# Dilated attention of a two-block layer stack: two small groups in one score tile by token class, 64x64 score matmuls, stacked values

## The chip, the cores and the metric

The kernel runs on one core of a Trainium2 chip. The metric is the device time of one execution in microseconds (us). The engines are called as the profile calls them: PE (the matrix engine; PEld is its weight load), DVE, ACT, POOL, and SP, which only issues transfers here.

## The reference, cut to what matters

Two blocks of two layers each run on 256 tokens of width 1024. The change is in the second block, whose layers are "hybrid": one projection feeds a gated convolution, an MLA attention of 8 heads and a dilated attention of 8 heads in three groups.

```python
DIL_PATTERNS = ((128, 1), (512, 4), (2048, 16))   # window, dilation
outs, lses = [], []
for gi, (window, dilation) in enumerate(DIL_PATTERNS):
    o_g, lse_g = dilated_group_attention(dq[:, :, gi], dk[:, :, gi], dv[:, :, gi], slopes[gi],
                                         dilation, window // dilation)
alpha = jax.nn.softmax(jnp.stack(lses, axis=0), axis=0)
o_c = jnp.sum(alpha[..., None] * jnp.stack(outs, axis=0), axis=0)
```

In a group of dilation d a query sees the keys whose distance is a multiple of d (at most 128 steps back), with a bias of minus slope times distance. Weighting the groups by the softmax of their log-sums equals one softmax over the scores of all three groups. With 256 tokens, a query of dilation 4 sees only keys of its own class mod 4 (64 tokens), and a query of dilation 16 only some of the same 64.

## The kernel before, in words

All activations are kept transposed (features on the 128 partitions, 256 tokens along the free side). A projection block is a 128x1024 piece of weights: SP fetches it into `raw`, ACT rounds it to `whi`, DVE makes the rest `wlo`, and PE runs 8 x 3 matmuls of 256 columns into a `G` slot (L513 to L515, in the function `run`). Values are made with tokens on the partitions by `run_tokens` (L572 to L574): two banks of `G`, one for each half of the tokens, from four weight blocks; ACT copies them to `dv` with `evac_tokens` (L1210). For the dilated heads, tokens are split by parity: ACT writes `dq`, `dk` even tokens first (L1573, L1574), and `run_tokens(by_parity=True)` reads every second token of `h` as its stationary operand.

The attention of a hybrid layer is one loop of 17 steps on PE (`for i in range(17)`), with blocks of other projections (`BESIDE[i]`) between: step i has the scores of head i (0 to 7 MLA, 8 to 15 dilated), the transposes of the weights of head i-1, and every second step `pair_outs`, weights times values for two heads. For a dilated head:

- POOL makes the biases (L489), one head ahead.
- `dil_scores` (L1089): group 0 needs every key, so 2 matmuls of 128x256; groups 1 and 2 need keys of the query's parity, so 2 of 128x128 each. The contraction is 64 deep; group 0 lies in one half of PE's rows and groups 1 and 2 in the other.
- DVE's `minima` (L2316) adds the bias, writes 1024 columns of `sn` and takes the minimum; ACT's `exps` (L1621) takes the exponential and its sum; DVE's `normalise` (L2330) scales.
- `to_keys` (L966) transposes 8 squares of 128x128, ACT copies them to `pt2` (L1660), and `pair_outs` (L1120) accumulates in `O`: for each of two heads, which take PE's left and right 64 columns, 2 matmuls of 256 columns for group 0 and 4 of 128 for groups 1 and 2.

A matmul on plain 32-bit operands (scores, values) runs on PE as two passes, and the trace has a row for each pass; transposes have one. After the loop come 36 merge blocks and the output projection. `settle` runs two small matmuls before the long runs. PE, DVE and ACT each work off their own list in the order of the code; semaphores join them.

Of the kernel before, what the change touches and what calls it, by code (L numbers as in the profile page):

```python
# [25 lines left out]
T = 256  # L26
P = 128
# [59 lines left out]
ORDER = (1, 0, 2)  # L87
SLOPES = [2.0 ** (-8.0 * (n + 1) / 24) for n in range(24)]

HYB_S = 4 + 4 + 8 + 24  # L90
# [34 lines left out]
for _f in range(FT):  # L125
# [10 lines left out]
WEIGHT_TILES = ((256, 768, 384, 896), (0, 512, 128, 640))  # L136
DIST = (slice(0, 512), slice(512, 768), slice(768, 1024))
PLACES = [((slice(0, T), slice(0, T)), (slice(T, 2 * T), slice(512, 768))),
          ((slice(0, P), slice(T, 384)), (slice(P, T), slice(768, 896))),
          ((slice(0, P), slice(384, 512)), (slice(P, T), slice(896, 1024)))]  # L140


def spans(i):

    return (slice(0, 512), slice(512, 1024)) if i >= 8 else (slice(0, P), slice(P, 384))


def even_odd(ap):

    return ap.rearrange("p (i two) -> p two i", two=2)  # L150


def score_uses(i):

    return 8 + min(i + 1, 8) + 3 * max(0, i - 7)
# [39 lines left out]
def build(nc, a, out):  # L195
# [8 lines left out]
    with ctx:  # L204
# [85 lines left out]
        dist = sb("dist", [P, 1024], stack=second)  # L290
# [10 lines left out]
        bias = sb("bias", [P, 1024], stack=second)  # L301
        pt2 = sb("pt2", [P, 2, 1024], stack=second)
        mn2 = sb("mn2", [P, 2, 2, 3], stack=second)
# [16 lines left out]
        u = yh[:, 4:12, :]  # L320
        s32 = sb("s32", [P, 32], stack=second)
# [13 lines left out]
        for n, t in (("o_dist", [P, 1024]), ("o_bones", [P, P]), ("o_lcs", [P, 2, 2, 16]),  # L335
                     ("o_rows", [P, LAYERS2, 2, 96])):
            sb(n, t, stack=mh_stack)
# [6 lines left out]
        for n, t in (("o2_dist", [P, 1024]), ("o2_bones", [P, P]), ("o2_lcs", [P, 2, 2, 16]),  # L344
                     ("o2_rows", [P, LAYERS2, 2, 96]), ("o2_dqk", [P, 24, T]), ("o2_dv", [P, 2, 1536])):
            sb(n, t, stack=sq2)
# [44 lines left out]
        bias_ready = sem("bias_ready")  # L391
        weights_ready = sem("weights_ready")
# [74 lines left out]
        def _(pool):  # L467
# [13 lines left out]
            with pool.Fori(0, LAYERS2) as l:  # L481
                for j in range(24):
                    head, grp = j // 3, ORDER[j % 3]

                    k = j - 3
                    pool.wait_ge(s_free, L1_S + l * HYB_S + (score_uses(8 + k // 3) - 2 + k % 3 if j >= 3 else 0))
                    c = 8 * grp + head
                    w = DIST[grp].stop - DIST[grp].start
                    pool.tensor_tensor(bias[:, DIST[grp]], dist[:, DIST[grp]], slopes[:, c:c + 1].broadcast_to([P, w]),  # L489
                                       ALU.mult).then_inc(bias_ready, 1)  # L490


        @block.tensor
        def _(pe):
# [58 lines left out]
            def run_tokens(b, g, j, b4=0, g4=0, by_parity=False):  # L553
# [3 lines left out]
                for jj, tt in {0: ((0, 0), (0, 1)), 1: ((1, 0), (1, 1)), 2: ((2, 0),), 3: ((3, 0), (2, 1), (3, 1))}[j]:  # L557
# [7 lines left out]
                    for kk in range(2):  # L565
                        k = 2 * jj + kk
                        if by_parity:
                            hh, hl = even_odd(h[:, k, 0:T])[:, tt, :], even_odd(h[:, k, T:2 * T])[:, tt, :]
                        else:
                            hh, hl = h[:, k, tt * P:(tt + 1) * P], h[:, k, T + tt * P:T + (tt + 1) * P]  # L570
# [375 lines left out]
            for l in range(LAYERS2):  # L946
# [118 lines left out]
                for j in range(12):  # L1065
                    run_tokens(B_HYB + H_DV + j // 4 * 4, G_HYB + H_DV + j // 4 * 4, j % 4, b4, g4, by_parity=True)
# [11 lines left out]
                def dil_scores(head):  # L1078
# [3 lines left out]
                    places = {0: (3 * p + 2 * e, 64 * e), 1: (3 * p + e, 64 - 64 * e), 2: (3 * p + 1 + e, 64 - 64 * e)}  # L1082
                    slots = {}
                    for grp, qt in ((1, 0), (0, 0), (1, 1), (0, 1), (2, 0), (2, 1)):
                        if qt == 0:
                            slots[grp] = use_s()
                        t, o = places[grp]
                        tile = slice(qt * P, (qt + 1) * P)
                        ins = pe.matmul(S[:, slots[grp], PLACES[grp][qt][0]], dqk[o:o + 64, t, tile],  # L1089
                                        dqk[o:o + 64, 12 + t, tile if grp else slice(0, T)], start=True, stop=True)  # L1090
                        if qt:
                            ins.then_inc(s_done, 1)

# [5 lines left out]
                def pair_outs(p):  # L1099
# [6 lines left out]
                    for grp in range(1 if last < 8 else 3):  # L1106
                        for kt in range(2):
                            for e in range(2):
                                i = 2 * p + e
                                to = O[64 * e:64 * e + 64, 0:T]  # L1110
                                if i < 8:
                                    to, v = to[:, P * kt:T], vm[:, kt, 64 * i:64 * i + 64]
                                    w = pt2[:, e, T * kt:T + P * kt]
                                elif grp == 0:
                                    v, w = dv[:, kt, 64 * (i - 8):64 * (i - 7)], pt2[:, e, 512 + T * kt:512 + T * (kt + 1)]
                                else:
                                    c = T * (grp - 1) + P * kt
                                    to, v = to[:, P * kt:P * kt + P], dv[:, kt, 512 * grp + 64 * (i - 8):512 * grp + 64 * (i - 7)]
                                    w = pt2[:, e, c:c + P]
                                ins = pe.matmul(to, v, w, start=(grp == 0 and kt == 0),  # L1120
                                                stop=(grp == (0 if last < 8 else 2) and kt == 1))
# [46 lines left out]
        def _(act):  # L1168
# [313 lines left out]
            for l in range(LAYERS2):  # L1482
# [87 lines left out]
                for j in range(24):  # L1570
                    done(H_DQ + j)
                    dq = even_odd(gslot(G_HYB + H_DQ + j))
                    act.activation(sq[:, j % 8, :].rearrange("p (two i) -> p two i", two=2), dq, ACT.Square).then_inc(d_sq, 1)  # L1573
                    freed(act.activation(dqk[:, j, :].rearrange("p (two i) -> p two i", two=2), dq, ACT.Copy), H_DQ + j)  # L1574
# [18 lines left out]

                for j in range(12):
                    if j % 4 == 2:
                        act.wait_ge(tok_done, l * 3 + (6 + j // 4 + 1))
                        evac_tokens(G_HYB + H_DV + j - 2, dv[:, :, (j - 2) * P:(j + 2) * P], 0)
                    done(H_DV + j)
                    if j % 4 == 3:
                        evac_tokens(G_HYB + H_DV + j - 3, dv[:, :, (j - 3) * P:(j + 1) * P], 1)  # L1600
# [39 lines left out]
                for i in range(18):  # L1640
# [16 lines left out]
                    if 1 <= i <= 16:  # L1657
                        for c0, c1 in ((0, 384),) if i <= 8 else ((0, 512), (512, 1024)):
# [4 lines left out]
                for mm in range(4):  # L1663
                    for q in range(9):
# [9 lines left out]
                        if q in (6, 8):  # L1674
                            m = 2 * mm + q // 8
                            act.wait_ge(m_ready, l * 8 + m + 1)
                            act.activation(mh[:, m, 0:T], mg[:, m % 2, :], ACT.Copy, scale=0.5).then_inc(m_hi, 1)
# [12 lines left out]
        def _(dve):  # L1690
# [430 lines left out]
            for l in range(LAYERS2):  # L2121
# [24 lines left out]
                def norm_tiles(ks):  # L2146
                    for k in ks:
                        dve.scalar_tensor_tensor(out=sq[:, k, :], in0=x[:, k, :], scalar=entry_gain(l, k), in1=rstd[:, :],
                                                 op0=ALU.mult, op1=ALU.mult).then_inc(t_ready, 1)
# [153 lines left out]
                def minima(i):  # L2303
                    s = i % 2
                    for grp in ORDER if i >= 8 else (0,):
                        slot = wait_s()
                        if i >= 8:
                            j = 3 * (i - 8) + ORDER.index(grp)
                            dve.wait_ge(bias_ready, l * 24 + j + 1)
                            add = bias[:, DIST[grp]]  # L2310
# [29 lines left out]
                def head_block(j):  # L2340
# [8 lines left out]
                    if kind == 1:  # L2349
# [3 lines left out]
                        freed(dve.tensor_tensor(ua[:, 2:2 + T], gslot(n), at[:, 0, :], ALU.mult), j)  # L2353
# [7 lines left out]
                    if kind == 2:  # L2361
                        done(j)
                        freed(dve.tensor_tensor(at[:, 1, :], gslot(n), at[:, 1, :], ALU.mult), j)
                    if kind == 3:
# [4 lines left out]
                        dve.scalar_tensor_tensor(out=at[:, 3, :], in0=at[:, 1, :], scalar=0.5, in1=at[:, 2, :],  # L2369
                                                 op0=ALU.mult, op1=ALU.mult).then_inc(a_ready, 1)  # L2370
                    next_lo(j)

                def pair_gate(p):
# [3 lines left out]
                    to, o = (hpair[:, :], O[:, 0:T]) if p < 4 else \  # L2377
                        (even_odd(hpair[:, :]), O[:, 0:T].rearrange("p (two i) -> p two i", two=2))
                    dve.scalar_tensor_tensor(out=to, in0=o, scalar=0.5, in1=z if p < 4 else even_odd(z), op0=ALU.mult,
# [22 lines left out]
                for mm in range(4):  # L2402
                    for q in range(6):
# [25 lines left out]
                        if q in (3, 5):  # L2429
                            m = 2 * mm + q // 4  # L2430
                            dve.wait_ge(m_hi, l * 8 + m + 1)
                            dve.scalar_tensor_tensor(out=mh[:, m, T:2 * T], in0=mg[:, m % 2, :], scalar=0.5,
                                                     in1=mh[:, m, 0:T], op0=ALU.mult, op1=ALU.subtract).then_inc(m_lo, 1)
# [12 lines left out]
def tables():  # L2446
# [12 lines left out]
    q = np.arange(T).reshape(P, 2).T  # L2459
    far = q[:, :, None] - q.reshape(-1)[None, None, :]  # L2460
    near = [np.where((far >= 0) & (far % d == 0) & (far // d <= back), far, MASKED) for d, back in zip(DIL, N_BACK)]
# [117 lines left out]
```

## Time and profile before

| what | value |
|---|---|
| median of 3 runs | 1452.4 us (1451.46 to 1452.83) |
| profiled execution, first to last instruction | 1450.8 us; no other time of its own is shown |
| PE, DVE, ACT, POOL busy | 99%, 72%, 58%, 6% of the span |
| TensorE clock granted | 0.999 of full speed, mean of the core |
| hybrid layer 0, from its first block to the next layer's | about 730 to 1092 us |
| hybrid layer 1 | about 1092 to 1450 us |

Times in the rows count from the first instruction. Matmuls overlap, so the length of one (0.28 us for 256 columns) is not what it costs: that is the distance from its start to the next start. Names like `S<-dqk` say what is written and read.

### The profile page before, as it was taken

To read this page: it belongs to the slowest core of one execution; us is meant where nothing else is said; L and a number is where in the kernel's file an instruction comes from. 1 tells how busy PE (TensorE), PEld (TensorE's weight loads), DVE (VectorE), ACT (ScalarE), POOL (GpSimd) and SP (SyncE) were. 2 spreads that over 40 slices of the span, in tenths; PEclk is the share of its full clock that TensorE was granted. 3 is DMA by queue.
4 is the path that set the end of the run, shared out by engine and by line. 5 is a ranking of instruction groups with operands and counts; after the bars stand their busy time and mean duration, and the time that the engine had idled before them with its cause. 6 is when DMAs were issued, how large, how long until landed. Compare 5 with 4: busy or idle time off the path is not lost.

```text
span 1450.8 us, 30291 instructions
## 1 busy us (share of the span) xinstructions
PE 1435.9 (99%) x11628; PEld 1365.4 (94%) x11628; DVE 1043.7 (72%) x1861; ACT 848.5 (58%) x1482; POOL 90.1 (6%) x136
## 2 busy tenths in 40 slices
PE   8999999999999999999999999999999999999999
PEld 6888999999979999999998989999999898999999
DVE  2878898888776668855666857876676684787664
ACT  4566666555556756445576766555566676656543
POOL 0111011110000000000020000320000000031000
PEclk9999999999999999999999999999999999999999
DMA  9966799996674366766663554336666355434663
GB/s 362 337 213 218 240 325 348 338 346 224 201 235 157 117 214 193 221 198 191 194 233 113 173 167 146 97 129 189 194 194 208 113 171 170 143 98 130 189 202 118
DMA packets 81186, 292.06 MB, mean 201 GB/s; under 512 B 9185, under 2 KB 10465, under 8 KB 80946
## 3 DMA queue, kind: packets, MB, share of 16 engines
q1 hardware_dynamic: 68274, 244.31, 51.8%
q0 software_dynamic: 11792, 42.77, 8.8%
q10 hardware_dynamic: 1008, 3.41, 0.7%
q8 instruction: 80, 1.31, 0.4%
q14 instruction: 32, 0.26, 0.1%
HBM read 289.40 MB, written 1.05 MB: 200 GB/s over the span
## 4 chain that ended last, share of the span: by engine, by line
PE 88%; DVE 7%; ACT 3%; issue 2%; DMA 1%; SPq 0%; DVEq 0%; ACTq 0%
PE G L513 22%; PE G L514 22%; PE G L515 22%; DVE wlo L1697 2%; PE G L572 2%; PE G L574 2%; PE G L573 2%; ACT whi L1177 1%; PE O L1120 1%; PE Tp L966 1%; PE Tp L908 1%; PE S L1019 1%; DVE aw L1705 1%; PE S L1089 1%; PE Tp L1044 1%
## 5 line engine op out<-in xcount | busy, mean ns | idle before, releaser
L1697 DVE TENSOR_TENSOR wlo<-raw,whi 128x1024 fp32r<-128x1024 f32 x444 | 545.9, 1232 | 253.8 <-ACT whi L1177 252.1
L1177 ACT ACTIVATE whi<-raw 128x1024 fp32r<-128x1024 f32 x444 | 468.7, 1058 | 217.8 <-PE G L515 157.4
L513 PE MATMUL G<-h,whi 128*128 128x256 f32 x2064 | 582.2, 282 | 0.3 <-DVE wlo L1697 0.2
L514 PE MATMUL G<-h,whi 128*128 128x256 f32 x2064 | 571.1, 277 | 0.0
L515 PE MATMUL G<-h,wlo 128*128 128x256 f32 x2064 | 571.0, 277 | 0.0
L513 PEld LDWEIGHTS G<-h,whi 128*128 128x128 f32 x2064 | 387.9, 188 | 5.6 <-issue 2.6
L514 PEld LDWEIGHTS G<-h,whi 128*128 128x128 f32 x2064 | 387.9, 188 | 0.7 <-issue 0.5
L515 PEld LDWEIGHTS G<-h,wlo 128*128 128x128 f32 x2064 | 387.7, 188 | 0.0
L1705 DVE CUSTOM_DVE_ANT_0 aw<-aw,cs,cols 128x1024 f32<-128x1024 f32 x80 | 101.4, 1279 | 0.0
L513 PE MATMUL G<-ah,whi 128*128 128x256 f32 x352 | 97.2, 276 | 0.0
L514 PE MATMUL G<-ah,whi 128*128 128x256 f32 x352 | 97.2, 276 | 0.0
L515 PE MATMUL G<-ah,wlo 128*128 128x256 f32 x352 | 97.2, 276 | 0.0
L513 PE MATMUL G<-yh,whi 128*128 128x256 f32 x288 | 80.1, 278 | 0.0
L514 PE MATMUL G<-yh,whi 128*128 128x256 f32 x288 | 79.7, 277 | 0.0
L515 PE MATMUL G<-yh,wlo 128*128 128x256 f32 x288 | 79.7, 277 | 0.0
L489 POOL TENSOR_TENSOR bias<-dist,slopes 128x256 f32<-128x256 f32 (+1 forms) x48 | 45.4, 961 | 532.8 <-DVE mn L2316 523.3
L572 PE MATMUL G<-whi,h 128*128 128x512 f32 x192 | 76.9, 401 | 0.9 <-ACT rv L1210 0.6
L472 POOL DMA_DIRECT2D aw<-in_ada x80 | 42.4, 530 | 543.8 <-DVE mod L1705 509.3
L574 PE MATMUL G<-wlo,h 128*128 128x512 f32 x192 | 75.7, 394 | 0.0
L573 PE MATMUL G<-whi,h 128*128 128x512 f32 x192 | 75.5, 393 | 0.0
L513 PEld LDWEIGHTS G<-ah,whi 128*128 128x128 f32 x352 | 66.1, 188 | 0.0
L514 PEld LDWEIGHTS G<-ah,whi 128*128 128x128 f32 x352 | 66.1, 188 | 0.0
(419 smaller groups left out, 2332.9 us busy)
## 6 DMA issues: line engine op xcount, KB each, us to landing
raw<-in_w SPq DMA_DIRECT2D x444, 512.0 KB, 4.0
aw<-in_ada POOLq DMA_DIRECT2D x80, 512.0 KB, 5.3
adaw<-in_ada SPq DMA_DIRECT2D x8, 1024.0 KB, 15.6
sn<-in_uq ACTq DMA_DIRECT2D x2, 768.0 KB, 4.4
x<-in_x SPq DMA_DIRECT2D x1, 1024.0 KB, 5.5
pt<-in_ukv ACTq DMA_DIRECT2D x2, 512.0 KB, 5.5
out<-x SPq DMA_DIRECT2D x4, 256.0 KB, 2.3
dec<-in_dec ACTq DMA_DIRECT2D x1, 512.0 KB, 7.2
```

Source lines behind the costliest of these rows:

```text
L472: pool.dma_start(aw[:, r % ADA_SLOTS, :], a["ada"][16 + r]).then_inc(ada_raw[r % ADA_SLOTS], 16)
L489: pool.tensor_tensor(bias[:, DIST[grp]], dist[:, DIST[grp]], slopes[:, c:c + 1].broadcast_to([P, w]), ALU.mult).then_inc(bias_ready, 1)
L513: pe.matmul(o, wh, mv[:, 0:T], start=(k == 0), stop=False)
L514: pe.matmul(o, wh, mv[:, T:2 * T], start=False, stop=False)
L515: ins = pe.matmul(o, wl, mv[:, 0:T], start=False, stop=(k == k_of - 1))
L572: pe.matmul(o, hh, wh, start=(k == 0), stop=False)
L573: pe.matmul(o, hl, wh, start=False, stop=False)
L574: ins = pe.matmul(o, hh, wl, start=False, stop=(k == KT - 1))
L908: ins = pe.matmul(to[:, o:o + P], w, moving[:, o:o + P], start=start, stop=True)
L1177: act.activation(whi[:, s, :], raw[:, s, :], ACT.Copy).then_inc(w_hi, 1)
L1697: dve.tensor_tensor(wlo[:, s, :], raw[:, s, :], whi[:, s, :], ALU.subtract).then_inc(w_lo, 1)
L1705: return dve.tensor_tensor_reduce(out=w, in0=w, in1=cs[:, :], scale=1.0, scalar=cols[:, C_ADAB + n:C_ADAB + n + 1], op0=ALU.mult, op1=ALU.add,
```

## The change

Tokens of a hybrid layer are kept by class mod 4 (four runs of 64) in `h`, not by parity. The query rows of one tile are then two classes of 64. Groups 1 and 2 each need only a 64x64 square for each class, so both go side by side into one 128x128 tile: group 1's square on the diagonal, group 2's off it. The parts:

- `dil_scores`: 4 matmuls of 64x256 and 8 of 64x64 in place of 2 of 128x256 and 4 of 128x128, and two `S` slots for a head in place of three.
- `sn` has 768 columns for a head and `to_keys` has 6 squares; `minima` has 4 reductions for a head, not 6.
- Values of groups 1 and 2 are stacked so that one contraction over 128 rows takes 64 rows of each: `values_out` copies half partitions of 512 columns. For group 2 the class pairs are crossed, for which POOL copies two shifted versions of `h` (`hy`) in each layer.
- `pair_outs`: 4 matmuls of 64x256 and 8 of 64x64 for two heads, in place of 4 of 64x256 and 8 of 64x128.
- The writes of DVE and ACT that go between the natural order and the class order step over 4 elements (`by_four`).

```diff
-HYB_S = 4 + 4 + 8 + 24
+HYB_S = 4 + 4 + 8 + 16
-WEIGHT_TILES = ((256, 768, 384, 896), (0, 512, 128, 640))
+WEIGHT_TILES = ((256, 640), (0, 384, 128, 512))
...
+                pool.wait_ge(blk_done, B_HYB + H_DQ + 7 + l * HYB_BLOCKS)
+                pool.wait_ge(h_ready, 40 + l * 8)
+                for c, o in ((0, 192), (64, 0), (128, T + 192), (192, T)):
+                    ins = pool.tensor_copy(hy[:, :, c:c + 64], h[:, :, o:o + 64])
+                ins.then_inc(hy_ready, 1)
...
-                        if by_parity:
-                            hh, hl = even_odd(h[:, k, 0:T])[:, tt, :], even_odd(h[:, k, T:2 * T])[:, tt, :]
+                        hh, hl = h[:, k, tt * P:(tt + 1) * P], h[:, k, T + tt * P:T + (tt + 1) * P]
+                        if crossed:
+                            hh, hl = (h[:, k, o + 64:o + 192] for o in (0, T)) if tt == 0 else \
+                                (hy[:, k, o:o + P] for o in (0, P))
...
-                    for grp, qt in ((1, 0), (0, 0), (1, 1), (0, 1), (2, 0), (2, 1)):
-                        if qt == 0:
-                            slots[grp] = use_s()
-                        t, o = places[grp]
-                        tile = slice(qt * P, (qt + 1) * P)
-                        ins = pe.matmul(S[:, slots[grp], PLACES[grp][qt][0]], dqk[o:o + 64, t, tile],
-                                        dqk[o:o + 64, 12 + t, tile if grp else slice(0, T)], start=True, stop=True)
+                    slots = [use_s(), use_s()]
+                    for qt in range(2):
+                        for a_ in range(2):
+                            q0 = qt * P + 64 * a_
+                            ins = pe.matmul(S[64 * a_:64 * a_ + 64, slots[0], PLACES[0][qt][0]],
+                                            dqk[far:far + 64, 3 * p + 2 * e, q0:q0 + 64],
+                                            dqk[far:far + 64, 12 + 3 * p + 2 * e, 0:T], start=True, stop=True)
+                        for t, swap in ((3 * p + e, 0), (3 * p + 1 + e, 1)):
+                            for a_ in range(2):
+                                q0, c = qt * P + 64 * a_, qt * P + 64 * (a_ ^ swap)
+                                keys = dqk[near:near + 64, 12 + t, q0:q0 + 64]
+                                ins = pe.matmul(S[64 * a_:64 * a_ + 64, slots[1], c:c + 64],
+                                                dqk[near:near + 64, t, q0:q0 + 64], keys, start=True, stop=True)
...
+                    for n in range(4 if last >= 8 else 0):
+                        for e in range(2):
+                            i = 2 * p + e - 8
+                            c = 512 + 512 * (n % 2) + 64 * i
+                            ins = pe.matmul(O[64 * e:64 * e + 64, 64 * n:64 * n + 64], dv[:, n // 2, c:c + 64],
+                                            pt2[:, e, 64 * n:64 * n + 64], start=False, stop=(n == 3))
...
+                    for half in range(2):
+                        n, r = 2 * half + tt, slice(64 * half, 64 * half + 64)
+                        kt, c = (tt, 512 + 512 * half) if grp == 1 else (half ^ tt, 1024 - 512 * half)
+                        act.activation(dv[r, kt, c:c + 512], G[r, (g + n) % 2, :], ACT.Copy)\
+                           .then_inc(slot_free[(g + n) % 4], 1)
...
-                    for grp in ORDER if i >= 8 else (0,):
+                    for grp in range(2 if i >= 8 else 1):
```

On PE, at a step of the loop that has `pair_outs` (head pair, then transposes of the head before, then scores of the next head, `S`), the list stood like this; a row is one matmul with its output's shape:

```order
L1120 MATMUL O<-pt,dv 64x256 x4
L1120 MATMUL O<-pt,dv 64x128 x8
L966 MATMUL Tp<-ident,sn 128x128 x8
L1089 MATMUL S<-dqk 128x128
L1089 MATMUL S<-dqk 128x256
L1089 MATMUL S<-dqk 128x128
L1089 MATMUL S<-dqk 128x256
L1089 MATMUL S<-dqk 128x128 x2
```

Now it stands like this:

```order
L1139 MATMUL O<-pt,dv 64x256 x4
L1144 MATMUL O<-pt,dv 64x64 x8
L981 MATMUL Tp<-ident,sn 128x128 x6
L1105 MATMUL S<-dqk 64x256 x2
L1114 MATMUL S<-dqk 64x64 x4
L1105 MATMUL S<-dqk 64x256 x2
L1114 MATMUL S<-dqk 64x64 x4
```

Nothing moved past anything else: the same three parts follow one another, with narrower second halves, two transposes fewer and the scores in smaller pieces.

On ACT, at the end of the value blocks (`dv` written from `G`) and before the loop, the list stood like this:

```order
L1210 ACTIVATE dv<-G 128x256 x2
L1177 ACTIVATE whi<-raw 128x1024
L1210 ACTIVATE dv<-G 128x256 x2
L1177 ACTIVATE whi<-raw 128x1024 x3
L1210 ACTIVATE dv<-G 128x256 x2
```

Now:

```order
L1628 ACTIVATE dv<-G 64x512 x2
L1201 ACTIVATE whi<-raw 128x1024
L1628 ACTIVATE dv<-G 64x512 x2
L1201 ACTIVATE whi<-raw 128x1024 x3
L1628 ACTIVATE dv<-G 64x512 x2
```

The copies stand in the same places, each over half the partitions and twice the columns; those of group 0 keep their old form.

## Rows read from the trace of the kernel before

**Rows 1.** The page: the span, and the busy time of the engines

```profile
span 1450.8 us, 30291 instructions
PE 1435.9 (99%) x11628; PEld 1365.4 (94%) x11628; DVE 1043.7 (72%) x1861; ACT 848.5 (58%) x1482; POOL 90.1 (6%) x136
```

**Rows 2.** Tile S: score passes of all 16 dilated heads (min/median/max ns)

```profile
L1089 PE MATMUL S<-dqk x192: 272/272/480, 909.6 to 1314.7; 64*128 64x128 f32 x128, 64*128 64x256 f32 x64
```

**Rows 3.** Timeline of PE: start, length, passes of one step's three parts

```profile
931.43 1.96 PE L1120 MATMUL O<-pt,dv 128*64 128x256 f32 x24
933.32 1.09 PE L966 MATMUL Tp<-ident,sn 128*128 128x128 f32 x8
934.35 1.16 PE L1089 MATMUL S<-dqk 64*128 64x128 f32 x12
935.43 0.39 PE L513 MATMUL G<-h,whi 128*128 128x256 f32 x1
```

**Rows 4.** Timeline of PE, values of an MLA pair and what follows

```profile
888.26 0.87 PE L1120 MATMUL O<-pt,vm 128*64 128x256 f32 x8
889.06 0.39 PE L513 MATMUL G<-h,whi 128*128 128x256 f32 x1
```

**Rows 5.** Timeline of PE, eight transposes and what follows

```profile
957.08 1.09 PE L966 MATMUL Tp<-ident,sn 128*128 128x128 f32 x8
957.93 0.36 PE L513 MATMUL G<-h,whi 128*128 128x256 f32 x1
```

**Rows 6.** Timeline of PE near the start: four column quarters of 512 columns

```profile
12.73 1.92 PE L692 MATMUL Tp<-adaw,silcb 128*32 128x512 f32 x16
```

**Rows 7.** Timeline of PE in a hybrid layer's value blocks, 27 rows

```profile
859.63 0.40 PE L572 MATMUL G<-whi,h 128*128 128x512 f32 x1
...
865.71 0.39 PE L574 MATMUL G<-wlo,h 128*128 128x512 f32 x1
```

**Rows 8.** The same in the retention layer, whose tokens aren't strided, 27 rows

```profile
395.42 0.39 PE L573 MATMUL G<-whi,h 128*128 128x512 f32 x1
...
401.37 0.39 PE L572 MATMUL G<-whi,h 128*128 128x512 f32 x1
```

**Rows 9.** Weight loads by form, busy us and mean ns: 835 to 873, then 400 to 500

```profile
L573 PEld LDWEIGHTS G<-whi,h 128*128 128x128 f32 x48 | 9.4, 195 | 1.6
...
L573 PEld LDWEIGHTS G<-whi,h 128*128 128x128 f32 x48 | 9.0, 188 | 2.0
```

**Rows 10.** Timelines of ACT and PEld where one value group follows another

```profile
859.83 0.66 ACT L1210 ACTIVATE dv<-G 128x256 f32<-128x256 f32 x2 [0.25 <-PE G L574]
...
860.81 0.20 PEld L572 LDWEIGHTS G<-whi,h 128*128 128x128 f32 x1
```

**Rows 11.** ACT by form, 909 to 963: copies of 512 columns out of PSUM

```profile
L1660 ACT ACTIVATE pt<-Tp 128x512 f32<-128x512 f32 x16 | 8.5, 585 | 0.3 <-PE Tp L966 0.3
```

**Rows 12.** Timeline of PE around the last head's transposes, layer 0

```profile
960.65 0.28 PE L515 MATMUL G<-h,wlo 128*128 128x256 f32 x1
961.69 1.09 PE L966 MATMUL Tp<-ident,sn 128*128 128x128 f32 x8 [0.76 <-DVE sn L2330]
```

**Rows 13.** Busy time of DVE in a window of the dilated heads, then by form

```profile
948.00:956.00 8.00, 7.82 (x41) 1.00 0.37 132
...
L2316 DVE CUSTOM_DVE_ANT_0 sn<-S,bias 128x128 f32<-128x128 f32 x32 | 7.9, 285 | 0.6 <-issue 0.6
L2330 DVE TENSOR_SCALAR sn<-sn,rj 128x512 f32<-128x512 f32 x16 | 7.2, 494 | 0.3
```

**Rows 14.** Busy time and count of PE in two windows of plain blocks

```profile
1094.00:1108.00 14.00, 14.00 (x121) 1.00 0.84 273
1000.00:1014.00 14.00, 14.00 (x126) 1.00 0.62 188
```

**Rows 15.** Layer entry: last of DVE's parts of h, PE's first block on h

```profile
742.25 1.43 DVE L2154 TENSOR_TENSOR h<-sq,h 128x256 fp32r<-128x256 f32 x4
...
746.74 0.28 PE L513 MATMUL G<-h,whi 128*128 128x256 f32 x1
```

More of the change, by code:

```diff
@@ L300, in build @@
         sn = sb("sn", [P, 2, 1024], stack=second)
-        bias = sb("bias", [P, 1024], stack=second)
+        bias = sb("bias", [P, 768], stack=second)
         pt2 = sb("pt2", [P, 2, 1024], stack=second)
-        mn2 = sb("mn2", [P, 2, 2, 3], stack=second)
+        mn2 = sb("mn2", [P, 2, 2, 2], stack=second)
+        sb("gap_mn2", [P, 4], stack=second)
         mj = sb("mj", [P, 2, 2], stack=second)
@@ L480, in _ @@
             pool.wait_ge(in_hyb, 64)
[L481 to L489, printed above, removed]
-                                       ALU.mult).then_inc(bias_ready, 1)
+            for l in range(LAYERS2):
+                pool.wait_ge(blk_done, B_HYB + H_DQ + 7 + l * HYB_BLOCKS)
[3 more added lines that the diff above has]
+                ins.then_inc(hy_ready, 1)
+                for head in range(8):
+                    taken_s = L1_S + l * HYB_S + (score_uses(7 + head) if head else 1)
+                    pool.wait_ge(s_free, taken_s - 1)
+                    pool.tensor_tensor(bias[:, 0:512], dist[:, 0:512], slopes[:, head:head + 1].broadcast_to([P, 512]),
+                                       ALU.mult).then_inc(bias_ready, 1)
+                    if head:
+                        pool.wait_ge(s_free, taken_s)
+                    far, near = (t[:, 512:768].rearrange("p (q c i) -> p q c i", q=2, c=2) for t in (bias, dist))
+                    for c in range(2):
+                        n = 8 + 8 * c + head
+                        pool.tensor_tensor(far[:, :, c, :], near[:, :, c, :],
+                                           slopes[:, n:n + 1].unsqueeze(2).broadcast_to([P, 2, 64]),
+                                           ALU.mult).then_inc(bias_ready, 1)
         @block.tensor
@@ L1105, in pair_outs @@
                     pe.wait_ge(t_free, t_base + (HYB_T - 24 + n))
[L1106 to L1121, printed above, removed]
+                    for kt in range(2):
+                        for e in range(2):
+                            i = 2 * p + e
+                            to = O[64 * e:64 * e + 64, 0:T]
+                            if i < 8:
+                                to, v = to[:, P * kt:T], vm[:, kt, 64 * i:64 * i + 64]
+                                w = pt2[:, e, T * kt:T + P * kt]
+                            else:
+                                v, w = dv[:, kt, 64 * (i - 8):64 * (i - 7)], pt2[:, e, T + T * kt:T + T * (kt + 1)]
+                            ins = pe.matmul(to, v, w, start=(kt == 0), stop=(last < 8 and kt == 1))
+                    for n in range(4 if last >= 8 else 0):
+                        for e in range(2):
+                            i = 2 * p + e - 8
+                            c = 512 + 512 * (n % 2) + 64 * i
+                            ins = pe.matmul(O[64 * e:64 * e + 64, 64 * n:64 * n + 64], dv[:, n // 2, c:c + 64],
+                                            pt2[:, e, 64 * n:64 * n + 64], start=False, stop=(n == 3))
                     ins.then_inc(o_done, 1)
@@ L2458, in tables, with near @@
     t["sbm"] = np.where(k2[None, :] + r[:, None] < q2[None, :], 0, -MASKED).astype(f)
-    q = np.arange(T).reshape(P, 2).T
-    far = q[:, :, None] - q.reshape(-1)[None, None, :]
-    near = [np.where((far >= 0) & (far % d == 0) & (far // d <= back), far, MASKED) for d, back in zip(DIL, N_BACK)]
-    t["dist"] = np.concatenate([near[0][0], near[0][1]] + [near[g][n][:, n * P:(n + 1) * P] for g in (1, 2) for n in range(2)],
-                               axis=1).astype(f)
-    t["slopes"] = np.tile(np.array(SLOPES, f)[None, :], (P, 1))
+    q = np.arange(T).reshape(64, 4).T.reshape(2, 2, 64)
+    rows_, own = q.reshape(2, P), np.stack([q, q[:, ::-1]]).reshape(2, 2, P)
+    def near(far, d, back):
+        return np.where((far >= 0) & (far % d == 0) & (far // d <= back), far, MASKED)
+    wide = [near(rows_[e][:, None] - q.reshape(-1)[None, :], DIL[0], N_BACK[0]) for e in range(2)]
+    half = r[:, None] // 64 == r[None, :] // 64
+    both = [np.where(half, near(rows_[e][:, None] - own[0, e][None, :], DIL[1], N_BACK[1]),
+                     near(rows_[e][:, None] - own[1, e][None, :], DIL[2], N_BACK[2])) for e in range(2)]
+    t["dist"] = np.concatenate(wide + both, axis=1).astype(f)
+    steep = np.array(SLOPES, f).reshape(3, 8)
+    low = np.broadcast_to(r[:, None] < 64, (P, 8))
+    t["slopes"] = np.concatenate([np.tile(steep[0], (P, 1)), np.where(low, steep[1], steep[2]),
+                                  np.where(low, steep[2], steep[1])], axis=1).astype(f)
     t["bones"] = np.kron(np.eye(2), np.ones((64, 64))).astype(f)
```

89 lines of the change are left out of this document (50 added, 39 removed).

## The prediction

> **What bounds the kernel now.** I read the page first: PE is busy for 99% of the span, DVE for 72%, ACT for 58% [rows 1]. Busy time overcounts PE, because matmuls overlap, so I took from the timeline the distance between starts. It shows PE working without a gap through the dilated heads: values of a pair, transposes, scores, next block, each starting where the last lets it [rows 3]. The list of who waited for whom has one wait of note on PE in the two hybrid layers: the transposes of the last head of layer 0 start 1.04 us after the matmul before them, and the releaser is DVE's `normalise` [rows 12]; 14 us for 126 starts make 0.11 the usual distance [rows 14]. So PE's own work sets the end, and what an edit takes off PE's stream comes off the time. DVE is the runner-up in the same place: busy 7.82 of 8 us from 948 to 956 [rows 13]. An edit that added DVE work there would cost; this one removes some.
>
> **How PE spends time on 32-bit operands.** Scores: 192 passes for 16 heads, 12 a head [rows 2], which is two passes for each of 6 matmuls. In columns streamed: group 0, in one half of the rows, 2 x 2 x 256 = 1024; groups 1 and 2, in the other half, 4 x 2 x 128 = 1024. The scores of a head take 1.08 us (934.35 to 935.43) [rows 3]. For the price of a column I compare two places where two heads stand side by side in the column halves: a dilated pair streams 2048 columns in each half and takes 1.89 us [rows 3], an MLA pair streams 2 x (256 + 128) = 768 and takes 0.80 us [rows 4]. Their difference is 1.09 us for 1280 columns, 0.85 ns each, and a fixed 1.89 - 2048 x 0.00085 = 0.15 us for going in and out. By it the scores' 1024 columns are 0.87 us, with 0.21 us fixed. Had the two row halves not run at the same time, it would be 1.74 us and more. So both kinds of overlap, of row halves and of column halves, are shown, but never all four quarters of the array at once.
>
> **The change part by part.**
>
> *Transposes.* Eight take 0.85 us (957.08 to 957.93) [rows 5], 0.106 each. Two fewer for each of 16 heads: 32 x 0.106 = **-3.4 us**.
>
> *Values of a pair.* Each column half streams 4 x 256 + 4 x 2 x 64 = 1536 columns, 512 fewer: 512 x 0.85 ns = 0.435 us a pair, 8 pairs: **-3.5 us**. No row has a steady stream of passes of 64 columns. The least is nothing, if such a pass costs as much as one of 128; more than the columns can't be saved, since the stationary operand is as wide as before. I take the columns, because 16 passes of 512 columns in four column quarters take 1.92 us [rows 6]; one after the other they would be 16 x 512 x 0.85 ns = 7 us, so four passes do start together, and the issue of a pass is far shorter than its streaming.
>
> *Scores.* If the four quarters run at once, the longest quarter is group 0's with 2 x 2 x 256 = 1024 columns, as before, and groups 1 and 2 (4 x 2 x 64 = 512 in a quarter) hide under it. Going in and out I price as for the values, whose stationary operand is 64 columns wide too: 0.87 + 0.15 = 1.02 us, 0.06 less than now; 16 heads: **-1.0 us**. The bounds are in the rivals.
>
> *Value blocks.* They now read `h` without a stride. With it 26 starts take 865.71 - 859.63 = 6.08 us [rows 7], 0.2338 each; in the retention layer the same matmuls without it take 401.37 - 395.42 = 5.95 us [rows 8], 0.2288 each, and the weight load itself is 195 against 188 ns [rows 9]. Per layer 12 x 12 matmuls, 288 in all: 288 x 0.0050 = **-1.4 us**. Nothing, if the cause is another.
>
> *The last head's wait* in layer 0. DVE loses two reductions of 128 columns a head and 256 columns of `normalise` (lengths 285 and 494 ns for 512 columns [rows 13]; I take 0.2 each, 0.6 in all), and ACT 256 columns of exponentials. PE comes some 0.5 us a head earlier (2 x 0.106 + 0.22 + 0.06), so DVE gains a little on it each step. Of 1.04 - 0.11 = 0.9 us I take off **-0.8 us**; bounds 0 and -0.9.
>
> *Value copies on ACT.* This one costs. Where group 2 follows group 1, PE needs the second bank back: ACT starts its two copies at 859.83, and they end 0.66 us later, at 860.49; PE's load for that bank starts at 860.81 [rows 10], so it is 0.3 us in hand. The new pair has 512 columns each. A copy of 512 columns is 585 ns long [rows 11]; the old ones are 0.38 long at a distance of 0.28, so the new distance is some 0.49 and the pair ends at 859.83 + 0.49 + 0.59 = 860.91, 0.1 us too late, 0.2 with the release. Once a layer: **+0.4 us**. After group 2 comes a whole block, which hides the last pair.
>
> *Costed at nothing.* POOL's copies for `hy` begin in the seventh query block and are wanted 25 blocks later; the bias work behind them on the same queue has 256 columns fewer a head than before. The steps over 4 elements lie on DVE and ACT. At layer entry DVE has its part of `h` done at 743.68 and PE starts on it at 746.74 [rows 15]: 3.1 us in hand; the eight strided writes (0.42 each) would have to take twice as long to use that up. Slots of `S`: two uses a head of three slots ask for less than three uses did.
>
> Sum: -3.4 - 3.5 - 1.0 - 1.4 - 0.8 + 0.4 = **-9.7 us**. The profiled span is 1450.8 and the median of the runs 1.6 longer; I carry the 1.6 over: 1452.4 - 9.7 = **1442.7 us**.
>
> [...]
>
> **The rivals.**
>
> *Issue binds.* Two passes in two halves of 128 columns stream in 128 x 0.85 = 0.109 us, 0.054 for each pass, the densest steady rate in these rows. If that is a floor, then the values of a pair gain nothing, and the 24 passes of a head's scores take 24 x 0.054 + 0.15 = 1.46 us, 0.38 more than now: 16 x 0.38 = +6.1. Sum -3.4 + 0 + 6.1 - 1.4 - 0.8 + 0.4 = +0.9: **1453.3 us**, no change. Against it: [rows 6].
>
> *Two quarters at a time.* The quarters' columns are 2 x 1024 + 2 x 512 = 3072; two streams share them as 1536, 1.31 + 0.15 = 1.46 us, again +6.1. Sum -3.4 - 3.5 + 6.1 - 1.4 - 0.8 + 0.4 = -2.6: **1449.8 us**.
>
> *Column halves queue up within one row half* (the other side). Group 0 then streams 2048 columns in a row: 1.74 + 0.15 = 1.89 us, +0.81 a head, +13.0. Sum -9.7 + 1.0 + 13.0 = +4.3: **1456.7 us**, slower. It decides from 1.08 + 8.7/16 = 1.62 us for a head's scores. For it: no row has it otherwise with a contraction of 64. Against it: with 128 rows column halves do overlap [rows 3].
>
> *The pace of plain blocks shifts.* In 14 us PE starts 126 matmuls in one stretch and 121 in another of the same kind, at the same clock [rows 14]: two paces 4% apart, and I don't know what picks one. If the 93 us of merge blocks of one layer fell to the slower: +3.7, **1446.4 us**. The stretch that is slow now (near 1068 to 1112) could gain 1.7 instead.
>
> **How the numbers follow.** Forecast 0.70, with a range of its own of 1440.5 to 1445; pace 0.09; two quarters 0.08; issue 0.06; slower 0.07. About 0.2% (2.9 us) is what a measurement can tell from no change: faster is below 1449.5, slower above 1455.3. Faster: 0.70 + 0.09 and 0.03 of the two-quarters case = 0.82; same: 0.05 + 0.06 = 0.11; slower 0.07. The range reaches from the forecast's low end with the slow stretch gained, 1440, to the two-quarters case, 1449.9; the other two are left out (0.13).
>
> **What the profile would show.** Scores: from the first of a head's 24 passes to the next block 1.02 us if I am right, 1.46 or 1.89 for the rivals, with groups 1 and 2 starting inside group 0's streaming. Values of a pair: 1.45 us; 1.89 if issue binds. Six transposes: 0.64 us. Value blocks: 0.229 us a start, and a gap of about 0.2 us at the first load for the second bank of group 2, put down to ACT's copy. The wait of 0.9 us before the last head's transposes in layer 0 gone. It goes wrong if PE waits somewhere in the loop for POOL's bias or ACT's copies, or if plain blocks in long stretches start at another distance than now.

## The result, and the profile after

The kernel after takes 1454.2 us (median of 20 runs, 1452.5 to 1459.3), the kernel before 1451.7 (20 runs, 1450.0 to 1453.8); the ratio is 1.0022, 95% interval 1.0014 to 1.0030. It is 0.2% slower. The 20 runs of after fall into two groups, 14 at 1452.5 to 1454.4 and 6 at 1457.8 to 1459.3; the trace is from the first. The forecast was 1442.7 us and a gain of 0.7%, with 1440.0 to 1449.9 as its range. The page of after:

```profile
span 1452.3 us, 30492 instructions
PE 1438.2 (99%) x11788; PEld 1362.6 (94%) x11788; DVE 1043.4 (72%) x1781; ACT 852.3 (59%) x1482; POOL 89.7 (6%) x144
```

PE is still busy for 99% of the span, as in [rows 1]. The timeline of PE at one step of the dilated loop answers to [rows 3]:

```profile
937.79 0.28 PE L530 MATMUL G<-h,wlo 128*128 128x256 f32 x1
937.99 1.08 PE L1139 MATMUL O<-pt,dv 128*64 128x256 f32 x8
938.91 0.63 PE L1144 MATMUL O<-pt,dv 128*64 128x64 f32 x16
939.47 0.87 PE L981 MATMUL Tp<-ident,sn 128*128 128x128 f32 x6
940.28 0.43 PE L1105 MATMUL S<-dqk 64*64 64x256 f32 x2
940.29 0.45 PE L1114 MATMUL S<-dqk 64*64 64x64 f32 x8
...
940.76 0.60 PE L1105 MATMUL S<-dqk 64*64 64x256 f32 x4
941.29 0.38 PE L528 MATMUL G<-h,whi 128*128 128x256 f32 x1
```

Values of a pair are 939.47 - 937.99 = 1.48 us (before 1.89), scores 941.29 - 940.28 = 1.01 (before 1.08). The small scores start 0.01 us behind the large ones, inside their streaming. The last head of layer 0 no longer waits; its rows answer to [rows 12], with six transposes in 961.94 - 961.31 = 0.63 us:

```profile
960.75 0.64 PE L1144 MATMUL O<-pt,dv 128*64 128x64 f32 x16
961.31 0.88 PE L981 MATMUL Tp<-ident,sn 128*128 128x128 f32 x6
961.94 0.37 PE L528 MATMUL G<-h,whi 128*128 128x256 f32 x1
```

The edited parts are near what was forecast for them, so the time went elsewhere. I looked for it with windows over stretches of plain blocks, where PE does nothing but matmuls of 256 columns: on `h` (200 to 240 and 590 to 630 us), on `ah` (295 to 335, the feed-forward of block 1) and on `yr` (510 to 530). Columns: sum, PE busy and its count of starts, granted clock, DMA share, GB/s. Before:

```profile
200.00:240.00 40.00, 40.00 (x355) 1.00 0.94 336
295.00:335.00 40.00, 40.00 (x355) 1.00 0.93 328
510.00:530.00 20.00, 20.00 (x172) 1.00 0.74 230
590.00:630.00 40.00, 40.00 (x355) 1.00 0.66 199
```

After:

```profile
200.00:240.00 40.00, 40.00 (x355) 1.00 0.93 334
295.00:335.00 40.00, 40.00 (x344) 1.00 0.89 319
510.00:530.00 20.00, 20.00 (x173) 1.00 0.66 213
590.00:630.00 40.00, 40.00 (x355) 1.00 0.64 210
```

The clock is 1.00 everywhere and nothing waits, but on `ah` 40 us hold 344 starts, not 355. This is in block 1, about 400 us ahead of the hybrid layers, where the edited matmuls stand. The matmuls themselves show it too. Tile `ah` (min/median/max ns), before and then after:

```profile
L513 PE MATMUL G<-ah,whi x352: 276/276/276, 283.6 to 722.9; 128*128 128x256 f32 x176
```

```profile
L528 PE MATMUL G<-ah,whi x352: 277/280/282, 285.1 to 729.1; 128*128 128x256 f32 x176
```

What changed for them is their address. `mark = sb("mark", [P, HYB_S])` is as long as the constant that the diff changes: 40 words became 32, and the allocator puts each tile behind the last, so every tile behind `mark` that is not moved more lies 32 bytes lower in its partition, `ah`, `oh` and `yr` of block 1 too (`yh` and `mh` lie 2080 and 1056 bytes lower, since `dist` and `bias` shrank). `h`, `whi` and `wlo` lie ahead of `mark` and stayed. The kernel before holds unused tiles (`gap_first`, `gap_second`, `gap_oh`, `gap_yh`), and with them `h`, `ah`, `oh`, `yr`, `yh` and `mh` all lie 192 bytes past `whi` modulo 256. The change adds one more of 16 bytes behind `mn2`, which it shortens too, but none behind `mark`. I summed over the trace the distance from each start on PE to the next, by moving operand:

| moving operand, matmuls (256 columns but for value blocks) | before, us | after | e1, below |
|---|---|---|---|
| h, 6288 | 734.1 | 735.5 | 733.1 |
| ah, 1056 | 119.7 | 123.9 | 119.7 |
| yh, 912 | 104.5 | 107.5 | 104.8 |
| mh, 383 | 44.9 | 45.5 | 43.7 |
| yr, 384 | 45.3 | 45.1 | 45.3 |
| oh, 192 | 22.2 | 23.1 | 22.2 |
| value blocks, 576 of 512 columns (288 of them in the hybrid layers) | 137.0 | 136.6 | 136.3 |
| transposes of sn | 20.9 | 17.3 | 17.3 |
| scores of the dilated heads | 17.5 | 16.2 | 16.2 |
| dilated values | 15.1 | 11.8 | 11.8 |

The last four rows gain 8.6 us in after; the first six lose 9.9.

### The profile page after: what moved, and what is told of

Same layout as the page of the kernel before. It is cut to its first block, busy times and chain, and to the rows that moved or that the text cites. A ratio compares the mean times of both kernels' runs of the same rounds, so it can differ in the third digit from the quotient of the medians.

```text
span 1452.3 us, 30492 instructions
## 1 busy us (share of the span) xinstructions
PE 1438.2 (99%) x11788; PEld 1362.6 (94%) x11788; DVE 1043.4 (72%) x1781; ACT 852.3 (59%) x1482; POOL 89.7 (6%) x144
## 4 chain that ended last, share of the span: by engine, by line
PE 91%; DVE 4%; ACT 3%; DMA 1%; issue 1%; SPq 0%; DVEq 0%; ACTq 0%
PE G L528 23%; PE G L530 22%; PE G L529 22%; PE G L587 2%; PE G L589 2%; PE G L588 2%; DVE wlo L1735 1%; PE Tp L981 1%; PE O L1139 1%; ACT whi L1201 1%; PE Tp L923 1%; DMA raw<-in_w 1%; PE S L1105 1%; PE S L1034 1%; DVE aw L1743 1%
## 5 line engine op out<-in xcount | busy, mean ns | idle before, releaser
L587 PE MATMUL G<-whi,h 128*128 128x512 f32 x176 | 70.5, 401 | 0.7 <-ACT rv L1234 0.3
L588 PE MATMUL G<-whi,h 128*128 128x512 f32 x176 | 69.1, 393 | 0.0
L589 PE MATMUL G<-wlo,h 128*128 128x512 f32 x176 | 69.0, 392 | 0.0
L530 PEld LDWEIGHTS G<-ah,wlo 128*128 128x128 f32 x352 | 66.2, 188 | 0.0
```

What stands on the lines that cost most here:

```text
L530: ins = pe.matmul(o, wl, mv[:, 0:T], start=False, stop=(k == k_of - 1))
```

## The experiments

Theory A: where a moving operand lies in its partition relative to the weights sets how fast plain blocks start. Rivals: B, the longer times are the program's (its new pieces, what runs beside it), not the addresses'; C, only the moves of 1024 bytes and more count; and, for the edited parts, the rivals of the prediction on quarters and issue.

**e1: after, with the 32 bytes put back.**

```diff
         mark = sb("mark", [P, HYB_S])
+        sb("gap_mark", [P, 8])
```

> The changed kernel with one unused tile of 32 bytes a partition behind the tile mark, nothing else. Theory A (address): the changed kernel made mark 32 bytes shorter, so that every tile behind it starts 32 bytes past a multiple of 64, and a plain matmul whose moving operand lies there starts every 117.3 ns instead of 113.3. Then ah, oh, yh and mh go back to the distances of before (ah 119.7 us in sum instead of 123.9, oh 22.2 for 23.1, yh 104.5 for 107.5), and with the value blocks some 9 to 11 us come back: 1443.5 to 1445, 0.994 of the kernel before. Theory B (order): the pace is set by what PE ran before a block, so the new score and value matmuls pick it: no change from 1454 within 1. Theory C (distance): what matters is the move by 1024 and 2048 bytes of the tiles behind dist and bias: ah and oh, which lie before them in another stack, would recover, yh and mh would not: about 1449.

1442.4 us (5 runs, 1440.4 to 1443.3), ratio 0.9933 [0.9919, 0.9947]. The one line is worth 12 us, 1 us more than theory A said; the `ah` row is back at 276/276/276 and 119.7 us. Theory B (1454) and theory C (1449, with `yh` not recovered; it is at 104.8) fall. This kernel is faster than before and after, and is the change as I had costed it.

**e2 and e3: before, moved by 32 and by 64 bytes.** The same line, with 8 words, then 16, in the kernel before.

> The kernel before with the same unused tile of 32 bytes behind mark, no other edit: all tiles behind it move from a multiple of 64 to 32 past one. Theory A: it gets slower by what the moving operands ah, yh, oh, mh lose, 8 to 11 us: 1460 to 1463. Theories B and C: no change, 1451.7 within 1.

> The kernel before with an unused tile of 64 bytes behind mark: every tile behind it moves, but stays on a multiple of 64. Theory A: no change, 1451.7 within 1.5. If any move of the tiles costs (each was placed by its full address), some 5 to 10 us slower.

e2: 1464.4, ratio 1.0085 [1.0071, 1.0098]. e3: 1470.9, ratio 1.0128 [1.0113, 1.0144]. Both are slower than forecast, e3 by 19 us. An unused gap alone makes the kernel slower, which B and C don't allow; but the form of A in which only multiples of 64 matter fell, since 64 bytes cost more than 32. Tile `ah` in e3:

```profile
L514 PE MATMUL G<-ah,whi x352: 280/283/283, 285.6 to 732.8; 128*128 128x256 f32 x176
```

Its stretches on `h`, which did not move, kept 355 starts in 40 us.

**e4 and e5: which distance.** In e4 the weights and all behind them move by 64 bytes and `h` stays; in e5 `h` moves too.

```diff
 e4:         raw = sb("raw", [P, 4, 1024])
+        sb("gap_whi", [P, 16])
 e5:         slopes = sb("slopes", [P, 24])
+        sb("gap_h", [P, 16])
```

> The kernel before with an unused tile of 64 bytes between raw and whi. Then whi, wlo and all tiles behind them move by 64 bytes, and h and x stay. In the kernel before whi and wlo start at a multiple of 128 and h, ah, yh, oh, yr, mh 64 past one; 64 bytes on for the moving tiles alone cost 19.5 us. Theory A1 (the two operands against each other): what counts is the distance of the moving operand from the weights modulo 128, 64 being fast and 0 slow. Then ah, yh and the others are fast again (113.3 ns a start), but h, with 6288 matmuls, is at distance 0: 120 ns a start instead of 114.3, +36: about 1487. Theory A2 (the moving operand alone must start 64 past a multiple of 128): h stays fast, the others are slow as in the last run: 1471.

> The kernel before with an unused tile of 64 bytes ahead of h: h, whi, wlo and all tiles behind them move by 64 bytes together, x and sq stay. Theory A1 (distance between the operands modulo 128): nothing changes, 1451.4 within 1.5. Theory A2 (place of the moving operand alone): all plain blocks are slow, +19.5 and h's +36: about 1507.

e4: 1481.7, ratio 1.0196 [1.0179, 1.0213]; now the matmuls on `h` are slow (762.5 us, +28 where A1 had +36), though `h` did not move, and in e5, where the weights moved as far but `h` with them, the window from 200 us is at 355 starts again: what counts there is where `h` lies relative to the weights. e5: 1463.3, ratio 1.0069 [1.0045, 1.0093]: far from the 1507 of absolute addresses, but 12 us from the no change that the distance alone gives. Windows of e4, then of e5:

```profile
200.00:240.00 40.00, 40.00 (x336) 1.00 0.93 317
295.00:335.00 40.00, 40.00 (x355) 1.00 0.96 344
...
590.00:630.00 40.00, 40.00 (x339) 1.00 0.69 214
```

```profile
200.00:240.00 40.00, 40.00 (x355) 1.00 0.96 341
295.00:335.00 40.00, 40.00 (x356) 1.00 0.93 331
...
590.00:630.00 40.00, 40.00 (x342) 1.00 0.62 195
```

In e5 the same code on the same operand starts 355 times in one window and 342 times in a later one. So A1 alone, with any modulus, does not give the time of e5. Against before, the trace of e5 loses 6.4 us between 565 and 730 us of before, in the long stretches on `h` and `ah` there, which start every 117.8 ns and not every 113.3, and 3.4 us in the hybrid layers.

**e6: after, with the 32 bytes put back for block 1 alone** (`gap_first` of 16 words in place of 8).

> The changed kernel with 32 bytes more at the head of the first block's tiles only (ah, oh, yr); the hybrid layers' tiles (yh, mh, dqk, dv) stay 32 bytes off. Address theory: the part of the loss that lies ahead of every edited instruction comes back and no more: ah 4.2, oh 0.9, and half of the sums around them, 5 to 6.5 us: 1448 to 1449. If the loss came from the hybrid layers' own instructions: no change from 1454.

1446.6 us, ratio 0.9957 [0.9940, 0.9973]: 7.6 of e1's 12 us, more than the 5 to 6.5 expected. In the trace `ah` and `oh` are back at 119.7 and 22.2 us. A large part of the loss lay in a block that the change does not touch. How large is not settled: it is 7.6 of 11.8 us by the medians, but between the traces of after and e1 only 5.0 of the 11.2 us lie in block 1 and 6.2 in the hybrid layers.

**e7: e1, with each 64x64 score matmul issued twice**; the second writes the same result to the same place.

```diff
-                        for t, swap in ((3 * p + e, 0), (3 * p + 1 + e, 1)):
+                        for t, swap in ((3 * p + e, 0), (3 * p + 1 + e, 1)) * 2:
```

> The changed kernel in the good layout (e1) with each of the eight 64x64 score matmuls of a dilated head issued twice, output unchanged. The second quarters then stream 1024 columns each, as many as group 0's. Theory Q4 (all four quarters at once, as the prediction had it): a head's scores stay at 1.01 us within 0.1, so 1442.4 to 1444. Two quarters at a time: 1024 columns more over two streams, 0.44 us a head, +7: 1449. Issue binds at 0.054 us a pass: 16 passes more a head, +0.87 us a head, +14: 1456.

1444.9 us, ratio 0.9948 [0.9931, 0.9964], 0.9 us above the range of Q4. A head's scores take 909.07 - 907.98 = 1.09 us with 40 passes; with 24 they took 1.01:

```profile
907.98 0.43 PE L1106 MATMUL S<-dqk 64*64 64x256 f32 x2
907.99 0.45 PE L1115 MATMUL S<-dqk 64*64 64x64 f32 x8
...
908.68 0.45 PE L1115 MATMUL S<-dqk 64*64 64x64 f32 x9
909.07 0.39 PE L529 MATMUL G<-h,whi 128*128 128x256 f32 x1
```

16 more passes add 0.08 us, 5 ns each, and the first four, one for each quarter, start 6 to 7 ns apart. Two quarters at a time (+0.44) and issue (+0.87) fall. At the prediction's 0.85 ns a column, which is an estimate, the 4096 columns of the four quarters are 3.5 us of streaming in 1.09 us, so all four quarters run at once.

**e8: before, moved by 128 bytes** (32 words behind `mark`).

> The kernel before with 128 unused bytes a partition behind `mark`, so that ah, oh, yr, yh and mh move by 128 bytes and keep their distance to whi and wlo mod 128. If only that distance counts: no change, 1451.6 us within 2, and matmuls on ah start 113.3 ns apart. If any move of those tiles costs, because the addresses before were chosen well: slower, as with 32 or 64 bytes, 1464 to 1471 us.

1473.1 us, ratio 1.0137 [1.0107, 1.0167]. My rule from e1 to e5, the distance mod 128, had no change here: `ah` has 342 starts in its 40 us. But 13.1 of the 21.9 us by which this trace is longer than that of before lie on `h`, which did not move, nor did the weights (747.2 us for 734.1), and the first long stretch on `yh` is as fast as in before, with 126 starts in 14 us. The windows on `h` and on `yh`:

```profile
590.00:630.00 40.00, 40.00 (x342) 1.00 0.64 200
742.00:756.00 14.00, 14.00 (x126) 1.00 0.77 289
```

So the distance of the moved tiles explains at most 8.4 us of e8 (their rows), and the loss on `h` is of the kind that e5 shows. The distance `ah` - `whi` is 63936 bytes in the kernel before. Mod 256 this and those of `h`, `oh`, `yr`, `yh` and `mh` are all 192, mod 512 they are 448 or 192. That made 256 the candidate for the period, which e12 tries.

**e9: before, value blocks of the dilated heads without the stride** (without `by_parity=True`: the values belong to other tokens).

> The kernel before, whose value blocks of the dilated heads read h without the stride of two; the values then belong to other tokens, so the output isn't the reference's. Starts of those 288 matmuls: from 233.8 to 228.8 ns if the stride is their cost (-1.4 us in all), unchanged if it is the place in the program.

The 288 value matmuls of the hybrid layers take 66.9 us, not 68.0: -1.1, where 288 x 5 ns are 1.4. They take 68.0 in seven other traces of the kernel before with the stride and with `h` at its old distance from the weights, so the stride is the cost. This one execution took 1457.8 us, for another reason: with every address and all code up to there as in before, its long stretches on `h` and `ah` from 566 to 728 us ran slow (342 starts in the window from 590, where before has 355).

**e10 and e11: e1 and e5 once more, to see what repeats.**

> The same program as e1, profiled once more. If the second pace (117.8 ns with the tiles at distance 64) is chosen by the program and its layout, each long stretch shows the pace that it had in e1, the one on yr 117.8. If it is chosen in each execution anew, as the same stretch in e7 (113.4) suggests, at least one long stretch differs between the two.

> The same program as e5, profiled once more. If the long stretches at 117.8 ns (567 to 731 and 738 to 760 us) are this layout's, they are there again and the span is 1462 or near. If chance, they stand elsewhere and the span differs by some us.

e10 (1442.0 us) is the same program as e1. Tile `yr` in e1, then in e10:

```profile
L529 PE MATMUL G<-yr,whi x96: 281/281/281, 509.2 to 542.7; 128*128 128x256 f32 x96
```

```profile
L529 PE MATMUL G<-yr,whi x96: 276/276/362, 507.6 to 540.0; 128*128 128x256 f32 x96
```

The stretch is fast in one execution and slow in the other (and `mh` the reverse, 276 in e1 and 281 in e10): a pace that is not fixed by the program. e11 (1463.1 us) repeats the slow stretch of e5 from 566 us on, and the times say that layout has a part in it: of 56 runs of the kernel before the slowest took 1456.8 us, while all 5 of e5 and e11 are above 1458.9. In e9 the same stretches are slow in the layout of before, so layout does not fix the pace, it makes the slow one more frequent.

**e12: before, moved by 256 bytes; e13: before, `h` and all behind it moved by 128.**

> The kernel before with 256 unused bytes a partition behind `mark`. The levels seen so far by a tile's distance behind the weights mod 256: 192 gives 113.3 ns a start, 160 gives 117.3, 224 gives 118.3, 0 gives 120.0, 64 gives 117.8. If 256 is the period: ah and oh at 113.3 again and 1451.6 us within 3. If each move of these tiles costs: 117 or more and 1464 us or more.

> The kernel before with 128 unused bytes ahead of h, so that h, the weights and all behind them move together and keep their distances. If the distance mod 256 is all: 1451.6 us within 3. If the place of the pair itself counts as well, as the 12 us of e5 let me think: 1458 us or more, with whole stretches at 116.7 or 117.8 ns (among them 566 to 731 us, as twice with 64 bytes).

e12: 1452.2, ratio 1.0008 [0.9993, 1.0023]; 256 bytes cost nothing in the whole, and `ah` is at 276 again:

```profile
L514 PE MATMUL G<-ah,whi x352: 276/276/276, 285.3 to 724.0; 128*128 128x256 f32 x176
```

This excludes that every move of these tiles costs. `oh` is not back, against what I expected: its matmuls are 281 ns long, and its row is 22.9 us for 22.2. e13: 1464.3, ratio 1.0086 [1.0069, 1.0103]. All distances were kept, and the time is again 12 us up, as in e5. Its trace, taken in its fastest execution (1458.8), has both long stretches on `h` at 113.3 ns a start; the matmuls on `h` lose 6.0 us all the same, 5.2 of them among the blocks of the hybrid layers.

Mean distance of starts over the long stretches (of 140 matmuls or more), by how far the moving tile lies behind the weights:

| distance mod 256 | seen in | ns a start |
|---|---|---|
| 192 | every tile in before, e1, e5, e7 and e9 to e13; `h` in all others but e4; `ah`, `oh`, `yr` in e6; all but `h` in e4 | 113.3 to 113.6, or 116.7 to 117.8, or between where the pace changes inside a stretch |
| 160 | all but `h` in after; `yh`, `mh` in e6 | 117.3 to 118.7 |
| 224 | all but `h` in e2 | 118.3 to 118.4 |
| 0 | the same in e3 | 119.9 to 120.0 |
| 64 | the same in e8 | 117.2 to 117.8; 113.3 in one of 8 stretches |
| 128 | `h` in e4 | 118.7 to 120.0 |

The cleanest evidence is two stretches that never show the second pace (116.7 or 117.8 ns) at 192. The first 528 matmuls on `ah` start every 113.3 or 113.4 ns in all 11 traces with `ah` at 192, and every 117.3 at 160, 118.3 at 224, 120.0 at 0 and 117.8 at 64, one trace each. The 960 matmuls on `h` from 175 us start every 113.3 ns in 14 traces at 192 and every 120.0 in e4. What the table does not settle is the period: the paces at 64 are found at 192 as well and the 120.0 at 0 also at 128, so a period of 128, with the slow pace more frequent in e8, fits these paces too. Only the whole times of e8 and e12 (+21 us, nothing) speak for 256.

## Why the prediction was wrong

The mechanisms of the edited parts were right, and so were their sizes to within 0.4 us each:

- *Transposes*: forecast -3.4, measured 17.3 - 20.9 = -3.6.
- *Values of a pair*: forecast 1.45 us a pair and -3.5, measured 1.48 and 11.8 - 15.1 = -3.3.
- *Scores*: forecast 1.02 us a head and -1.0, measured 1.01 and 16.2 - 17.5 = -1.3. The rivals with two quarters, with queueing column halves and with issue are excluded by this row and e7.
- *Value blocks and value copies on ACT*: forecast -1.4 + 0.4. In the hybrid layers' 288 matmuls they make -0.7 together in e1, where the lost stride alone made -1.1 in e9. In after only -0.4: the 48 matmuls whose stationary operand comes from `hy`, which lies in `yh` and moved with it, start 233.2 ns apart there and 229.4 in e1. The copies cost what was forecast, though the pair is 1.21 us long and not the 1.08 of the working: ACT has it from 867.07 to 868.28, PE's next load starts at 868.33, and the next two distances are 0.33 and 0.34 us in place of 0.23, 0.2 us a layer. From after:

```profile
867.79 0.39 PE L588 MATMUL G<-whi,h 128*128 128x512 f32 x1
868.01 0.40 PE L589 MATMUL G<-wlo,h 128*128 128x512 f32 x1
868.34 0.50 PE L587 MATMUL G<-whi,yh 128*128 128x512 f32 x1
868.68 0.40 PE L588 MATMUL G<-whi,yh 128*128 128x512 f32 x1
```

- *The last head's wait*: forecast -0.8, gone (0.9). It stands in the row on `h`, which is 1.0 lower in e1.

The step that failed is *Costed at nothing*, and with it the term of zero for every block that the diff does not touch. It went through queues, covers and slots, and not through what else depends on the constant `HYB_S`: the length of `mark`, and by it the address of every tile behind. Its consequence was in the rivals, as *The pace of plain blocks shifts*, but with a chance of 0.09, confined to the 93 us of merge blocks of one layer and sized +3.7 us. In fact the tiles `ah`, `oh`, `yh` and `mh` all lost their place, in both blocks: e1 against after, 1454.2 - 1442.4 = 11.8 us. In the table, whose traces of after and e1 are 11.2 us apart, 9.6 lies on the rows of these four (1.2 us of that is `mh` in e1 at 113.6 ns by chance, see e10, and not at 116.7 as in before), and the `h` row, whose operands did not move, has 2.4. I wrote that I didn't know what picks between the two paces, and took the unknown for small. The last line of the prediction names plain blocks that start at another distance as a sign of its being wrong, and that sign came. With the 32 bytes put back the forecast of 1442.7 meets 1442.4, in part by luck: it started from 1452.4, while before took 1451.4 beside e1, so that the gain is 9.0 us and not 9.7, and the 1.2 us on `mh` were no part of the forecast. The low end of its range, 1440, does not come out of its terms either: 1440.5 less the 1.7 of the slow stretch is 1438.8.

The argument on chances had the same flaw: a known unknown that bears on all plain matmuls (1071 of 1451 us, the first six rows of the table) was priced by one stretch where it might strike, where 4% over the 2543 plain matmuls on `ah`, `yh`, `mh` and `oh` (291 us) is already 11.7 us, more than the whole gain.

What stays open: why a distance of 192 is a good one and whether 64 is as good; what picks the second pace; why moving the pair of `h` and weights together by 64 or 128 bytes costs 12 us (e5, e13); and why `h` loses 13.1 us in e8. The matmuls on `h` take 1.4 us more in after than in before although neither they nor the weights moved, and 2.4 more than in e1, since the wait that is gone stood in the same row, in pieces of 0.1 to 0.6 us all over the program; I put that down to the second pace, and no run shows it.

## What to carry to other kernels

When a change alters a constant, follow it into the sizes of all tiles, and print the addresses of before and after: a gap of the lost length behind the shrunken tile is one line and was worth 11.8 us here. Where the bounding engine's matmuls change their own length (276 to 280 ns) in a part that nobody edited, look at where the operands lie before you look at the code; but profile a second execution too, since 276 and 281 ns also come in two executions of one program (`yr` in e1 and e10). An unused tile in a kernel may be there for this: work out what distance it keeps. Then try gaps of 32 to 256 bytes for each large moving tile, and look at the length of its matmuls, which shows the pace before the total does.

## What the runs showed of the hardware

The spacing of 256-column matmuls at a full clock (granted 1.00 in every window) depends on where the moving operand lies relative to the weights in the partition: 113.3 ns at best, 120.0 at worst, 6%. In the kernel before, a gap of 32, 64 or 128 bytes behind `mark` costs 13, 19 or 21 us (e2, e3, e8; in e8 13.1 us of it by the traces on `h`, which did not move), one of 256 nothing (e12). With nothing but an unused gap added, PE starts 335 matmuls in 40 us on `ah` (e3), not 355. Why the place counts is not shown: no run separates the reads of PE from what DVE and ACT read and write meanwhile.

At the good distance there is a second pace (116.7 or 117.8 ns). In the 15 traces the pace changes in none of the 153 stretches of 72 and more of these matmuls on one tile that have no distance over 121 ns between starts, and it can differ between two executions of one program (`yr` 281 ns long in e1, 276 in e10). The kernel before has it too, on `yr` (117.8) and `mh` (116.7).

With a contraction of 64 and 64 output rows, all four quarters of the array stream at once (e7: by the estimate of 0.85 ns a column 3.5 us of streaming in 1.09 us), and 16 more passes of 64 columns beside streams of 256 cost 0.08 us.
